# Differential attention in a two-layer decoder trunk: where the per-head statistics, the output transposes and the output slabs stand in the attention steps

## The reference, cut to what matters

```
q = rms_norm((h @ w_q).reshape(b, s, 8, 2, 64))          # 8 heads, 2 components of 64
for i in range(4):                                       # query blocks of 128
    sc = einsum(q_block_i, k[:, :q_end]) * scale         # two score maps a head, causal
    p = softmax(where(causal, sc, -1e30))
    a = p[component 0] - lam * p[component 1]
    outs.append(einsum(a, v))                            # v_dim 128 a head
o = rms_norm(concatenate(outs), sub_norm) * (1 - lam_init)   # per head
x = x + o.reshape(b, s, 1024) @ w_o
```

## Time and profile before

| | us |
|---|---|
| median of 3 runs | 1119.24 |
| the profiled execution | 1118.9 |
| its span, first to last instruction | 1117.1 |
| PE busy | 1097.7 (98%) |
| DVE busy | 793.6 (71%) |
| ACT busy | 478.9 (43%) |
| first scores of the loop | 641.2 |
| last values of the loop | 742.7 |
| first chunk of output slab 4 | 758.8 |

### The profile page before, as it was taken

The page is one execution under the profiler, slowest core; times in us unless marked ns, Lnnn a source line. Parts: engine busy times, 40 slices in busy tenths (PEclk is TensorE's granted clock), DMA queues, the critical chain, the costliest instruction groups (busy, mean ns, idle before and its releaser), DMA issues.

```text
span 1117.1 us, 13426 instructions
## 1 busy us (share of the span) xinstructions
PE 1097.7 (98%) x5176; PEld 903.8 (81%) x5176; DVE 793.6 (71%) x988; ACT 478.9 (43%) x695; POOL 78.6 (7%) x58
## 2 busy tenths in 40 slices
PE   9999999999999999999999998899999999999998
PEld 7788888888888888888888876677878888888887
DVE  5766554787787787688664678946668678678686
ACT  6221224353353353355532366834544344344343
POOL 0000012000000000002510211013100000000000
PEclk9999999999999999999999999999999999999999
DMA  7433463314315315201322300142323423414302
GB/s 189 93 98 99 131 208 95 113 38 155 109 38 173 91 41 186 76 1 57 114 94 76 113 1 20 58 151 78 113 74 110 117 76 116 127 59 139 88 1 75
DMA packets 144752, 105.90 MB, mean 95 GB/s; under 512 B 12592, under 2 KB 121136, under 8 KB 144688
## 3 DMA queue, kind: packets, MB, share of 16 engines
q1 hardware_dynamic: 143648, 105.03, 30.7%
q10 hardware_dynamic: 1040, 0.00, 0.1%
HBM read 102.93 MB, written 2.10 MB: 94 GB/s over the span
## 4 chain that ended last, share of the span: by engine, by line
PE 94%; DVE 3%; issue 1%; ACT 1%; POOL 0%; ACTq 0%; DVEq 0%; POOLq 0%
PE ps L588 31%; PE ps L615 27%; PE ps L470 18%; PE ps L675 10%; PE ps L700 2%; PE ps L761 1%; DVE nmax L1512 1%; PE ps L739 1%; PE ps L751 0%; ACT w_hi L843 0%; PE ps L523 0%; DVE h L1548 0%; PE ps L720 0%; PE ps L557 0%; PE ps L649 0%
## 5 line engine op out<-in xcount | busy, mean ns | idle before, releaser
L588 PE MATMUL ps<-h,w_hi 128*128 128x512 f32 x1024 | 316.3, 390 | 0.0
L615 PE MATMUL ps<-w_hi,h 128*128 128x512 f32 x896 | 277.6, 389 | 0.8 <-ACT kv L932 0.8
L588 PEld LDWEIGHTS ps<-h,w_hi 128*128 128x128 f32 x1024 | 191.6, 188 | 39.3
L470 PE MATMUL ps<-h,w_hi 128*128 128x512 f32 x640 | 199.1, 392 | 3.4 <-DVE w_lo L1148 1.6
L588 PE MATMUL ps<-h,w_lo 128*128 128x512 f32 x512 | 199.4, 389 | 0.0
L615 PEld LDWEIGHTS ps<-w_hi,h 128*128 128x128 f32 x896 | 168.2, 188 | 36.0 <-issue 1.0
L615 PE MATMUL ps<-w_lo,h 128*128 128x512 f32 x448 | 174.4, 389 | 0.0
L470 PEld LDWEIGHTS ps<-h,w_hi 128*128 128x128 f32 x640 | 118.8, 188 | 28.6 <-DVE h L1548 1.8
L928 ACT ACTIVATE w_hi<-b_raw 128x1024 fp32r<-128x1024 f32 x80 | 82.1, 1055 | 137.6 <-PE ps L588 78.1
L470 PE MATMUL ps<-h,w_lo 128*128 128x512 f32 x320 | 124.7, 390 | 0.0
L1249 DVE TENSOR_TENSOR w_lo<-b_raw,w_hi 128x1024 fp32r<-128x1024 f32 x80 | 95.9, 1224 | 27.4 <-ACT w_hi L928 27.4
(11 more groups left out here) (133 smaller groups left out, 1196.7 us busy)
## 6 DMA issues: line engine op xcount, KB each, us to landing
b_raw<-in_w_down SPq DMA_DIRECT2D x64, 512.0 KB, 4.5
w_raw<-in_w_up SPq DMA_DIRECT2D x64, 512.0 KB, 4.1
w_raw<-in_a_w_in SPq DMA_DIRECT2D x23, 512.0 KB, 3.8
w_raw<-in_w_kv SPq DMA_DIRECT2D x16, 512.0 KB, 3.7
w_raw<-in_a_w_out SPq DMA_DIRECT2D x8, 512.0 KB, 4.2
w_raw<-in_w_q SPq DMA_DIRECT2D x8, 512.0 KB, 3.5
w_raw<-in_w_o SPq DMA_DIRECT2D x8, 512.0 KB, 4.0
kv<-in_x SPq DMA_DIRECT2D x4, 512.0 KB, 6.5
```

Of the source, the lines that this page charges most:

```text
L470: last = nc.tensor.matmul(ps[:, bank, :], w[:, s, k * P:(k + 1) * P], src(half, k), start=(k == 0 and i == 0), stop=(k == KC - 1 and i == 2))
L588: last = nc.tensor.matmul(ps[:, v % 4, :], w[:, s_, k * P:(k + 1) * P], h_of[inp][:, half, k, :], start=(k == 0 and i == 0), stop=(k == KC ...
L615: last = nc.tensor.matmul(ps[:, CHAIN[p][tb], :], op[half][:, k, tb * P:(tb + 1) * P], w[:, s_, cols], start=(FRESH[p] and k == 0 and i == ...
```

## The change

- `WO_EARLY`: only slab 0 is split inside the loop, at (2, 3). ACT writes slab 1's hi half in step (7, 3); the rest of slabs 1 to 3 is split behind the loop.
- `WO_FILL`: chunks 0 to 5 of slab 0 move to (3,1), (3,3), (4,2), (5,2), (6,2), (7,2).
- PE: `weights_T(n)` goes ahead of `queries_T` and `out_T`. All of slab 1 moves behind the last values; out_T(7) moves in between the chunks of slab 2.
- ACT: the square of o is taken from the copy in SBUF, behind the evacuation; `values` of the next head waits for the copy alone. `out_hi(h)` moves from the end of (h+1, 3) to (h+2, 0) behind the square; `take_q` goes ahead of the evacuation, `q_hi` behind it.
- DVE: `weights(n + 1)` goes ahead of `out_ms`; `out_lo(h)` moves from the start of (h+2, 0) to the end of (h+2, 1). The ratio in `weights` is a scalar_tensor_tensor with one pointer in place of a tensor_scalar with two.

```diff
@@ -48,8 +48,8 @@
 Q_BANK = (4, 5, 0, 1, B_Q, B_Q, B_Q, B_Q)
 QT_BANK = (B_T, B_O, B_T, B_O, B_T, B_T, B_T, B_T)
 STEPS = 4 * H
-WO_FILL = {(3, 1): (0,), (3, 2): (1,), (4, 1): (2,), (5, 1): (3,), (6, 1): (4,), (7, 1): (5,)}
-WO_EARLY = {(2, 3): 0, (3, 3): 1, (4, 2): 2, (5, 2): 3}
+WO_FILL = {(3, 1): 0, (3, 3): 1, (4, 2): 2, (5, 2): 3, (6, 2): 4, (7, 2): 5}
+WO_EARLY = (2, 3)
 K_T_AFTER = 7
 X_BANK = (4, 5, 6, 7, 2, 3, 4, 5)
 WO_BANK = (B_Q, 1, 2, 3, 0, 1, 2, 3)
@@ -756,7 +756,7 @@
                 h, i = divmod(n, 4)
                 pe.wait_ge(s_ev, n + 1)
                 if i == 0 and h:
-                    pe.wait_ge(s_oc, 2 * h)
+                    pe.wait_ge(s_oc, 2 * h - 1)
                 for j in range(i + 1):
                     last = nc.tensor.matmul(ps[:, B_O, i * P:(i + 1) * P], a_T[n % 2][:, j * P:(j + 1) * P],
                                             v_all[:, j, h * P:(h + 1) * P], start=(j == 0), stop=(j == i))
@@ -797,29 +797,24 @@
                 if (h, i) == (3, 1):
                     pe.wait_ge(s_qsq, 16)
                 if (h, i) in WO_FILL:
-                    project_out(0, WO_FILL[h, i])
-                if (h, i) == (H - 1, 2):
-                    pe.wait_ge(s_exp, 2 * STEPS - 2)
-                    project_out(1, range(0, 3))
-                if (h, i) == (H - 1, 3):
-                    project_out(1, range(3, 5))
+                    project_out(0, (WO_FILL[h, i],))
                 if n:
                     values(n - 1)
+                weights_T(n)
                 if i == 2 and h < 4:
                     queries_T(4 + h)
                 if i == 3 and h:
                     out_T(h - 1)
-                weights_T(n)
 
             pe.wait_ge(s_exp, 2 * STEPS)
-            project_out(1, range(5, 6))
-            project_out(2, range(0, 2))
             values(STEPS - 1)
-            project_out(2, range(2, 6))
+            project_out(1, range(0, 6))
+            project_out(2, range(0, 3))
+            out_T(H - 1)
+            project_out(2, range(3, 6))
             project_out(3, range(0, 6))
             for m in range(ACC):
                 project_out(m, range(6, 7))
-            out_T(H - 1)
             for m in range(ACC):
                 project_out(m, range(7, 8)).then_inc(s_used, 1)
             for m in range(ACC, KC):
@@ -1081,9 +1076,13 @@
                 act.wait_ge(s_pv, 4 * h + 4)
                 if h:
                     act.wait_ge(s_oT, h)
+                nc.scalar.activation(o_sb, ps[:, B_O, :], ACT.Copy).then_inc(s_oc, 1)
+
+            def square_o(h):
+                act.wait_ge(s_oc, 2 * h + 1)
+                if h:
                     act.wait_ge(s_oms, h)
-                nc.scalar.activation(o_sb, ps[:, B_O, :], ACT.Copy).then_inc(s_oc, 1)
-                nc.scalar.activation(o_sq, ps[:, B_O, :], ACT.Square).then_inc(s_oc, 1)
+                nc.scalar.activation(o_sq, o_sb, ACT.Square).then_inc(s_oc, 1)
 
             def out_hi(h):
                 act.wait_ge(s_oT, h + 1)
@@ -1108,16 +1107,24 @@
                     exps(n + 1)
                 if i == 0 and h:
                     copy_o(h - 1)
+                if i == 3 and h < 3:
+                    take_q(5 + h)
+                if n == STEPS - 1:
+                    split(S_WO + 1)
+                evacuate(n)
+                if i == 0 and h:
+                    square_o(h - 1)
+                if i == 0 and h >= 2:
+                    out_hi(h - 2)
                 if i == 2 and h < 4:
                     q_hi(4 + h)
-                if i == 3 and h < 3:
-                    take_q(5 + h)
-                evacuate(n)
-                if i == 3 and h:
-                    out_hi(h - 1)
-                if (h, i) in WO_EARLY:
-                    split(S_WO + WO_EARLY[h, i])
+                if (h, i) == WO_EARLY:
+                    split(S_WO)
+            split(S_WO + 2)
+            out_hi(H - 2)
             copy_o(H - 1)
+            square_o(H - 1)
+            split(S_WO + 3)
             out_hi(H - 1)
 
             for m in range(KC):
@@ -1519,8 +1526,8 @@
                 dve.wait_ge(s_exp, 2 * m + 2)
                 V.reciprocal(rinv[:, b, 0:1], rsum[:, h % 2, i, 1:2]).then_inc(s_sc, 1)
                 dve.wait_ge(s_sc, 2 * m + 1)
-                V.tensor_scalar(rinv[:, b, 1:2], rinv[:, b, 0:1], rsum[:, h % 2, i, 0:1], lams[:, 5:6],
-                                ALU.mult, ALU.mult).then_inc(s_sc, 1)
+                V.scalar_tensor_tensor(rinv[:, b, 1:2], rinv[:, b, 0:1], lams[:, 5:6], rsum[:, h % 2, i, 0:1],
+                                       ALU.mult, ALU.mult).then_inc(s_sc, 1)
                 dve.wait_ge(s_sc, 2 * m + 2)
                 if m >= 2:
                     dve.wait_ge(s_T, m - 1)
@@ -1570,27 +1577,30 @@
             q_stats(4)
             for n in range(STEPS):
                 h, i = divmod(n, 4)
-                if i == 0 and h >= 2:
-                    out_lo(h - 2)
                 if n + 2 < STEPS:
                     row_max(n + 2)
+                if n + 1 < STEPS:
+                    weights(n + 1)
                 if i == 1 and h:
                     out_ms(h - 1)
-                if n + 1 < STEPS:
-                    weights(n + 1)
                 if i == 1 and h < 4:
                     q_norm_part(4 + h)
+                if i == 1 and h >= 2:
+                    out_lo(h - 2)
                 if i == 2 and h:
                     out_norm(h - 1)
                 if i == 2 and h < 4:
                     q_lo(4 + h)
                 if i == 3 and h < 3:
                     q_stats(5 + h)
-                if (h, i) in WO_EARLY:
-                    split(S_WO + WO_EARLY[h, i])
+                if (h, i) == WO_EARLY:
+                    split(S_WO)
+            split(S_WO + 1)
+            split(S_WO + 2)
             out_lo(H - 2)
             out_ms(H - 1)
             out_norm(H - 1)
+            split(S_WO + 3)
             out_lo(H - 1)
 
             for m in range(KC):
```

## The result

The changed kernel takes 1132.37 us (median of 6 runs, 1130.29 to 1134.61) against 1119.13 before (6 runs, 1118.78 to 1120.17): ratio 1.0118, 95% interval 1.0108 to 1.0128. It is slower, as forecast, but by 13.2 us and not 5.4; the time lies 5.4 above the upper end of the range. The profiled execution took 1131.93, its span (first to last instruction) 1130.1.

A forecast was written before the change was run, and what follows sets the result against it. DVE was taken to bound the kernel from head 4 on, with PE's matmul stream following attention. Terms 1.5 (to S(7,3)), 0.0 and 3.95 (behind the loop) made +5.4 us: 1124.6, stated as 1124.5, range 1121.0 to 1127.0.

The forecast's parts named there:

- Exponentials: ACT, step (h,2), heads from 4 on: end 2.96 us after the 512-column score group S(h,3) starts.
- both waits: PE in late heads: 1.5 us before S(h+1,0) for exponentials, 2.0 before slab 0's chunk for out_lo; 4.1 in head 7.
- the period: Late heads, start of S(h,3) to start of S(h+1,3): 11.9 us; three heads cost +4.2 against 31.54.
- the middle stretch: From S(7,3) to the first output chunk behind the last values: 11.05 us against 11.04, no difference.
- the tail: Behind the loop, first chunk to slab 4's first chunk: eight more chunks +5.5, out_T(7)'s wait of 1.56 gone, net +3.95.
- the gain up to S(4,3): Heads before the late ones: waits removed or shortened by the reordering, -1.4, -0.9 and -0.4 us.
- Rival 3: PE's clock falls in or after the longer waits of late heads and head 7: 1141 or 1127.5 us; chance 0.05 together.
- all late heads at 1.2 GHz: Clock-fall case: 8.8 us of PE work a head becomes 17.6, 5.7 over the period, three times: 1141 us.
- only behind the 4.1: Clock-fall case: after head 7's 4.1 us wait alone, some 3 us of matmuls double: 1127.5 us.
- Not slower (1): Late heads: out_lo is done when PE reaches the chunk, so its wait does not bind; period 10.0, 1117 us; chance 0.08.
- The cheaper tail (2): Head 7's last steps: waits shrink once nothing fills them, at most 3 us less, 1121.5 to 1123; chance 0.14.
- Late slabs (4): Behind the loop: slab 3 or 6 lands late behind the bigger loads, 1126 to 1128 us; chance 0.06.

## Why the prediction was wrong

**Right, with sizes.** The mechanism and its place: the chunk of slab 0 waits for an out_lo that DVE does last in the step before. Exponentials, out_lo, both waits, and at full clock the period, the middle stretch and the tail, came within 0.4 us each, the gain up to S(4,3) was 2.7 forecast and 2.7 measured, and the whole schedule at full clock 1123.5 against 1124.5; the 1.0 is three heads at 0.2, the tail's 0.3 and a rest of 0.1. One part of the 2.7 was read wrongly: the wait ahead of the query transposes in (3,2) was to stay near its 1.30 (half of it covered, 0.66 taken back by the later out_lo), and is 1.75, up to the end of out_lo. The sum came out all the same. Rival 3 doesn't name this wait, though three of the profiles above lose the clock behind it (at 1.75 twice, at 0.99 with out_lo in its old place). Slab 3 and the later loads cost nothing: slab 4's wait is 0.43 against 0.39. That the splits which left the loop bought nothing in the late heads of the changed kernel fits DVE's idle time there (4.5 of 13.25).

**Wrong.** The step that failed is the clock of PE, rival 3: chance 0.05, nothing in the sum, and outside the range. In its place the runs showed 8.9 us of the 13.2, from a mean clock of 0.87 to 0.64 in the heads with the long waits. The rival was laid out with the right waits (1.5, 2.0, 4.1) and the Trainium skill's rule at its side (TensorE: Matmul & The Clock Gate, the section on HAM oscillation), and then given almost nothing, because "all slices are at 2.4 GHz now, across waits up to 1.56". The sum prices a wait as the time that PE stands and no more. The reason reads one profiled execution as if it were the kernel, from a row that can't show a short loss. The times did not say so: of the executions of the kernel before that ran beside these experiments, 47 of 68 had a mean clock of 1.000 and took 1118.92 on average, 17 had 0.998 and took 1120.11, and 4 had 0.997 and took 1120.92. Three in ten lost some of the clock, for 1.2 to 2.0 us. The highest of the three times shown ahead of the prediction, 1120.17 beside a lowest of 1118.9, is where such an execution lies; no clock was read for it. That a kernel so near the edge would go beyond it with longer and more frequent waits could have been expected; it is an argument, not a reading. The size was off too: the case "all late heads at 1.2 GHz" (1141) and "only behind the 4.1" (1127.5) left out what happened, and the range, said to take in this rival's milder end, stops at 1127.0, below both. The price behind the 4.1 was right (some 3, and 3.1 measured); the late heads were priced at 5.7 each, and lost 1.5, 1.5 and 2.3, a part of each head; 8.9 in all by the medians.

The general form of the slip: a wait was priced as the time that PE stands. The work behind it at half speed cost twice the whole net of the schedule (8.9 against 4.3). By the Trainium skill's rule (same section) the clock falls in waits between short bursts; this trace agrees in kind, with 0.87 to 0.64 in the heads that have the waits and 1.00 before and after them.

**The rivals.** Not slower (1) fell: out_lo ended when laid out. The cheaper tail (2) fell: 11.02 and 18.87. Late slabs (4) fell. The clock (3) is what decided.

## What to carry to other kernels

A wait on a loop's critical engine has to be looked up twice: once for the time it stands, once for what the clock does to the work behind it; and the spread of the times, beside the clock of each execution, tells how near the kernel is to that edge before anything is changed. When a consumer moves one step, follow what its producer now stands behind: here one operation put last in a DVE step and its reader first in the next PE step turned a change worth 6.7 us into a loss of 13.2. Reorders of an engine that is not the bound are worth what the bound lets through (2.0 us alone, 5.3 with the rest of the change in place), so undo parts in the final kernel as well as adding them to the first, one at a time.

## What the runs showed of the hardware that was not expected

- Adding work made the kernel faster. Matmuls by zero in the waits (59 of them, 512 columns each) took 8.9 us off, and they held the clock although their weights were all zero: it was 1.000 in all five executions.
- The clock fell in some executions of a kernel and not in others: the kernel with out_T(7) moved had five of ten at 1.000 (mean 1117.17), three at 0.996 (1119.07). In each profile that shows it, the fall lies behind or within a stretch where PE stood: 0.99 to 1.75 us ahead of the query transposes, the long waits of the changed kernel's late heads, and head 7's last steps.
- The cost is not the same for an equal loss of clock. From 1.000 to 0.998 the kernel before lost 1.2 us, the one with PE busy in heads 4 to 7 lost 1.35 (1124.80 against 1123.45, two executions each), the one with out_hi and out_lo back 0.7 (1114.44 against 1113.77, two each). Where in the program the fall lies decides what it costs; which stretch it was in those executions is open, since only profiled ones were read.
